# A decoder layer on one core: its opening cut into feature pairs, its last two products turned to tokens on partitions

## The chip, the cores and the metric

The kernel runs on one core of a Trainium2 chip. The metric is the device time of one launch in microseconds (us), with all inputs in HBM at its start and the result in HBM at its end.

## The reference, cut to what matters

One layer over 512 tokens and 1024 features, in float32:

```python
h = rms_norm(x, norm_mix[i])
proj = (h @ w_in[i])                       # 3840 columns: attention A, HGRN2 B, MoBA C
x = x + concat(ya, yb, yc) @ w_out[i]
x = x + GatedMLP(DWConv3(rms_norm(x, norm_ffn) @ w_up)) @ w_down
x = x + sigmoid(rms_norm(x, norm_ple) @ w_pg) * (p[i] @ w_pe)
return rms_norm(x, norm_final)
```

w_pe is 256 x 1024 and w_pg 1024 x 1024. rms_norm divides a token's row by the root of its mean square and multiplies by a gain per feature.

## The kernel before, in words

Each product is made of three: operands are split into a rounded part (`w_hi`, `h_hi`) and the remainder (`w_lo`, `h_lo`), and hi x hi, hi x lo and lo x hi are summed in a PSUM bank (lines 466 to 468). ScalarE (ACT) makes the hi parts, VectorE (DVE) the lo parts. Weights come in "units" of 512 KB (8 blocks of 128 x 128, `UNITS`): SyncE loads a unit into one of three `raw` slots, when the unit three before has its lo part; ACT and DVE split it two units ahead; TensorE (PE) runs its 24 matmuls of 512 columns (tokens); DVE "takes" the bank. Features lie on partitions: a unit's output is 128 features x 512 tokens.

**Order.** Every engine runs a list written out by hand, `beside_unit(u)` on ACT and DVE. Units 0 to 29 are w_in, 30 to 37 w_out, 38 to 81 w_up (in a loop), 82 to 105 w_down, 106 and 107 w_pe, 108 to 115 w_pg. PE uses two accumulator banks in turn, so unit u waits until unit u-2 is taken.

**Opening.** SyncE loads x in four tiles of 128 tokens, then units 0, 1, 2. PE transposes x in 32 transposes of 128 x 128 (L650); DVE and ACT copy them to `x_t`. ACT makes 8 `h_hi` (L839) and DVE 8 `h_lo` (L1167) for all of x, and unit 0 runs. ACT sums the squares of each token's row (L1033, four times), DVE takes the root of them in 13 small steps (`rstd_of_rows`, L1183 to L1195) and spreads it on a diagonal (L1200); PE turns this into `r_row` during unit 1 (L486). Only then can unit 0 be taken (L1217): the norm's root multiplies the product. The first four units (z) each need a take, three activations and three DVE steps (L1272 and on).

**Last stage.** Units 106 and 107 (`p @ w_pe`) give 8 banks, which ACT copies to `pe_out`. For each of the 8 w_pg units, 128 features x 512 tokens: DVE multiplies with `r_row` (L1217), ACT takes the sigmoid (L912), DVE multiplies with `pe_out` and adds to `x_t` (L1312, L1314), PE transposes the result to rows (L778, four transposes in the next unit), DVE multiplies with the final gain (L1320), and ACT squares four pieces (L971). The last unit runs in two halves of 256 tokens (`take_half` and on). Then, by halves: mean, Ln, Exp, three DVE steps, and the scaling of whole rows by DVE (L1591) and ACT (L1140), and four output DMAs of 512 KB (L456).

## Time and profile before

| | |
|---|---|
| median of 3 runs | 750.8 us (748.54, 750.8, 750.8) |
| the profiled execution, its own time | 747.16 us |
| its span, first to last instruction | 745.4 us |
| around the span | 1.76 us |
| mean granted TensorE clock | 0.993 |
| busy: PE, weight loads, DVE, ACT, POOL | 723.8, 592.6, 453.2, 314.2, 122.4 us |

Times in the rows below are us from the start of the span. A timeline row is start, duration, engine, line, operation, out<-in, count, and in brackets how long the engine had been idle and who released it. The granted clock is 1.00 at TensorE's 2.4 GHz and 0.50 at 1.2 GHz. An operation's duration ends when its result is there; a pipelined engine starts the next one some 0.1 us earlier (ACT, DVE), and TensorE 0.16 us earlier.

### The profile page before, as it was taken

To read this page: it belongs to the slowest core of one execution; us is meant where nothing else is said; L and a number is where in the kernel's file an instruction comes from. 1 tells how busy PE (TensorE), PEld (TensorE's weight loads), DVE (VectorE), ACT (ScalarE), POOL (GpSimd) and SP (SyncE) were. 2 spreads that over 40 slices of the span, in tenths; PEclk is the share of its full clock that TensorE was granted. 3 is DMA by queue.
4 is the path that set the end of the run, shared out by engine and by line. 5 is a ranking of instruction groups with operands and counts; after the bars stand their busy time and mean duration, and the time that the engine had idled before them with its cause. 6 is when DMAs were issued, how large, how long until landed. Compare 5 with 4: busy or idle time off the path is not lost.

```text
span 745.4 us, 10529 instructions
## 1 busy us (share of the span) xinstructions
PE 723.8 (97%) x3935; PEld 592.6 (80%) x3935; DVE 453.2 (61%) x705; ACT 314.2 (42%) x545; POOL 122.4 (16%) x99
## 2 busy tenths in 40 slices
PE   5999999998999999999999999999999999999993
PEld 4778777877888878778888888888888888888883
DVE  4754779748866645576767676676763333324555
ACT  7652214255665634444333343433332223226344
POOL 1030000025655432201011101101110001000000
PEclk9999999999999999999999999999999999999998
DMA  8333221312222102333332323333215332333202
GB/s 263 113 89 112 58 58 57 118 53 85 86 86 86 58 29 85 113 107 92 97 102 85 112 84 107 90 94 103 85 49 163 98 105 79 99 113 113 86 0 114
DMA packets 121745, 69.44 MB, mean 93 GB/s; under 512 B 2658, under 2 KB 118450, under 8 KB 121706
## 3 DMA queue, kind: packets, MB, share of 16 engines
q1 hardware_dynamic: 119982, 65.72, 29.4%
q10 hardware_dynamic: 1724, 3.19, 1.3%
q8 instruction: 26, 0.43, 0.2%
q14 instruction: 13, 0.11, 0.0%
HBM read 66.77 MB, written 2.13 MB: 92 GB/s over the span
## 4 chain that ended last, share of the span: by engine, by line
PE 88%; DVE 5%; ACT 3%; issue 1%; DMA 1%; SPq 0%; POOL 0%; DVEq 0%; ACTq 0%
PE bank L466 26%; PE bank L468 26%; PE bank L467 26%; PE bank L506 2%; PE bank L606 2%; DVE w_lo L1161 2%; PE bank L588 2%; PE bank L574 1%; DMA raw<-in_w_in 1%; ACT w_hi L834 1%; PE bank L576 1%; DVE h_lo L1167 1%; DVE x_t L1252 1%; PE bank L540 1%; ACT scratch L852 1%
## 5 line engine op out<-in xcount | busy, mean ns | idle before, releaser
L466 PE MATMUL bank<-h_hi,w_hi 128*128 128x512 f32 (+1 forms) x664 | 264.3, 398 | 2.6 <-DVE h_lo L1167 2.6
L468 PE MATMUL bank<-h_hi,w_lo 128*128 128x512 f32 (+1 forms) x664 | 257.8, 388 | 0.0
L467 PE MATMUL bank<-h_lo,w_hi 128*128 128x512 f32 (+1 forms) x664 | 257.7, 388 | 0.0
L834 ACT ACTIVATE w_hi<-raw 128x1024 fp32r<-128x1024 f32 (+1 forms) x116 | 120.8, 1042 | 288.2 <-PE bank L468 288.1
L1161 DVE TENSOR_TENSOR w_lo<-raw,w_hi 128x1024 fp32r<-128x1024 f32 (+1 forms) x116 | 144.7, 1247 | 113.0 <-ACT w_hi L834 112.8
L466 PEld LDWEIGHTS bank<-h_hi,w_hi 128*128 128x128 f32 x664 | 125.1, 188 | 28.6 <-DVE w_lo L1161 2.8
L468 PEld LDWEIGHTS bank<-h_hi,w_lo 128*128 128x128 f32 x664 | 125.1, 188 | 26.2
L467 PEld LDWEIGHTS bank<-h_lo,w_hi 128*128 128x128 f32 x664 | 125.3, 189 | 24.2 <-issue 1.0
L1647 POOL TENSOR_SCALAR probs<-probs,row_inv 128x512 f32<-128x512 f32 (+3 forms) x48 | 66.0, 1379 | 148.4 <-DVE row_inv L1432 148.1
L466 PE MATMUL bank<-act_hi,w_hi 128*128 128x512 f32 x176 | 68.6, 389 | 0.0
L468 PE MATMUL bank<-act_hi,w_lo 128*128 128x512 f32 x176 | 68.5, 389 | 0.0
L467 PE MATMUL bank<-act_lo,w_hi 128*128 128x512 f32 x176 | 68.5, 389 | 0.0
L1217 DVE TENSOR_TENSOR scratch<-bank,r_row 128x512 f32<-128x512 f32 x54 | 37.3, 690 | 45.5 <-PE bank L468 43.7
L1655 POOL TENSOR_TENSOR conv_v<-conv_g,conv_v 128x512 f32<-128x512 f32 x22 | 28.3, 1288 | 213.1 <-DVE conv_v L1290 213.1
L1625 POOL TENSOR_TENSOR sumsq<-sumsq,scratch 128x512 f32<-128x512 f32 x14 | 18.1, 1295 | 146.8 <-ACT scratch L852 146.8
L985 ACT ACTIVATE probs<-probs,row_min 128x512 f32<-128x512 f32 (+3 forms) x48 | 27.0, 563 | 35.2 <-DVE row_min L1426 35.0
L1426 DVE CUSTOM_DVE_ANT_0 probs<-bank,bias 128x512 f32<-128x512 f32 (+3 forms) x48 | 23.5, 489 | 27.9 <-PE bank L576 18.5
L839 ACT ACTIVATE h_hi<-x_t,vec_cols 128x512 fp32r<-128x512 f32 x24 | 16.6, 719 | 53.3 <-DVE x_t L1252 53.3
L467 PEld LDWEIGHTS bank<-act_lo,w_hi 128*128 128x128 f32 x176 | 33.0, 188 | 6.9
L468 PEld LDWEIGHTS bank<-act_hi,w_lo 128*128 128x128 f32 x176 | 33.0, 188 | 6.8
L466 PEld LDWEIGHTS bank<-act_hi,w_hi 128*128 128x128 f32 x176 | 33.0, 188 | 6.8
L993 ACT ACTIVATE probs_t<-bank 128x512 f32<-128x512 f32 (+3 forms) x48 | 20.6, 429 | 9.5 <-PE bank L588 8.9
(186 smaller groups left out, 791.7 us busy)
## 6 DMA issues: line engine op xcount, KB each, us to landing
raw<-in_w_up SPq DMA_DIRECT2D x44, 512.0 KB, 3.6
raw<-in_w_in SPq DMA_DIRECT2D x30, 512.0 KB, 3.7
raw<-in_w_down SPq DMA_DIRECT2D x16, 512.0 KB, 3.2
raw<-in_w_out SPq DMA_DIRECT2D x8, 512.0 KB, 3.3
raw<-in_w_pg SPq DMA_DIRECT2D x8, 512.0 KB, 3.3
bias<-bias_table ACTq DMA_DIRECT2D x6, 512.0 KB, 3.7
raw<-in_w_down SPq DMA_DIRECT2D x8, 384.0 KB, 2.8
x_rows<-in_x SPq DMA_DIRECT2D x4, 512.0 KB, 5.8
```

What stands on the lines that cost most here:

```text
L466: pe.matmul(bank, hi, x_hi, start=first, stop=False)
L467: pe.matmul(bank, hi, x_lo, start=False, stop=False)
L468: return pe.matmul(bank, lo, x_hi, start=False, stop=last)
L834: act.activation(w_hi[:, u % SPLIT, 0:nk * ncol], raw[:, u % RAW, 0:nk * ncol], ACT.Copy)\
L985: act.activation(probs[:, n % PROBS, 0:keys], probs[:, n % PROBS, 0:keys], ACT.Exp, scale=-1.0, bias=row_min[:, n:n + 1], accum_out=row_su ...
L993: act.activation(probs_t[:, n % TURNED, 0:keys], turned[n % 2][:, 0:keys], ACT.Copy).then_inc(probs_t_ready, 1)
L1161: dve.tensor_tensor(w_lo[:, u % SPLIT, 0:nk * ncol], raw[:, u % RAW, 0:nk * ncol], w_hi[:, u % SPLIT, 0:nk * ncol].bitcast(F32), ALU.subtr ...
L1217: return dve.tensor_tensor(out, bank, r_row[:, :], ALU.mult)
L1426: dve.tensor_tensor_reduce(out=probs[:, n % PROBS, 0:keys], in0=score[n % 2][:, 0:keys], in1=bias[:, pair % 2, head % 2, SEQ - keys:SEQ], ...
L1625: pool.tensor_tensor(sumsq[:, :], sumsq[:, :], scratch[:, 2 + f % 2, :], ALU.add).then_inc(sumsq_ready, 1)
L1647: pool.tensor_scalar(probs[:, n % PROBS, 0:keys], probs[:, n % PROBS, 0:keys], row_inv[:, n:n + 1], None, ALU.mult)\
L1655: pool.tensor_tensor(conv_v[:, j % 3, :], conv_g[:, j % 3, :], conv_v[:, j % 3, :], ALU.mult).then_inc(prod_ready, 1)
```

## The change

**Opening.** x is loaded in four pairs of feature blocks (all 512 tokens x 256 features, rows of 1 KB in HBM), each followed by the same two blocks of units 0, 1 and 2 (128 KB each). The identity moves to ACT's DMA queue. TensorE first runs 7 matmuls on a zeroed tile, then transposes pair 0, runs two more of those, and then, pair by pair, the products of units 0, 1, 2 side by side in three banks, with the transposes of the next pair between. `h_hi` and `h_lo` are made straight from the transposes' banks. Groups 0 to 7 go over four banks instead of two (`bank_of`, `frees`). The row squares, all four, come on ACT after the last pair, then the splits of units 3, 4 and 5, then `r_row` (in unit 3's last block). The conv transposes and the bias look-up move two units later.

**Last stage.** w_pe and w_pg become moving operands and the activations stationary: output is 128 tokens x 512 features. 8 pieces of w_pe (6 matmuls each) are each followed by the transposes of one `x_t` block into `y_rows` (`turn_rows`), copied by DVE and ACT in turn. The norm's root is then one number per token and partition, so the sigmoid applies it as its scale and reads the bank directly. w_pg is loaded as 8 units of 256 x 512, five of which have split tiles of their own (`pg_hi`, `pg_lo`). 8 tiles `g` follow: tokens g % 4, feature half g // 4; the last in two halves of 256 columns. There are no transposes in this stage and the squares are taken from `y_rows`. Roots of tokens 0 to 383 are found on DVE in 13 steps (`root_of`), that of the last 128 with Ln and Exp as before. Rows leave in four DMAs, the last split in two. The gain row is loaded at unit 85 instead of unit 111, into `conv_v`'s place.

The diff, cut to its core; of the parts that replace others mostly the added lines stand:

```diff
-for _f in range(KT):
-    _unit("w_pg", 0, KT, _f * P)
-    _group("ple", _f)
+for _c in range(2):
+    for _k0 in range(0, KT, 2):
+        _unit("w_pg", _k0, 2, _c * 512, 512)
...
+def bank_of(group):
+    return group % 4 if group < WIDE else group % 2
+def frees(group):
+    return None if group < 4 else group - 4 if group < WIDE + 2 else group - 2
+def split_at(u):
+    return {1: None, 2: None, 3: 6, 4: 7, 5: 8, 6: None}.get(u, u + 2)
...
-            for t in range(TT):
-                sp.dma_start(x_rows[:, t, :], a["x"][0, t * P:(t + 1) * P, :]).then_inc(x_in[t], 16)
-                if t == 0:
-                    sp.dma_start(square[:, 0:P], a["c_square"][:, 0:P]).then_inc(ident_in, 16)
-            load_unit(0)
-            load_unit(1)
+            for j in range(PAIRS_K):
+                cols = slice(2 * j * P, (2 * j + 2) * P)
+                sp.dma_start(x_rows[:, :, cols], a["x"][0, :, cols].rearrange("(t p) c -> p t c", p=P)).then_inc(x_in[j], 16)
+                for u in range(FIRST):
+                    name, _, _, c0, ncol = UNITS[u]
+                    sp.dma_start(raw[:, u, cols].rearrange("p (k c) -> p k c", c=ncol),
+                                 w_dram[name][cols, c0:c0 + ncol].rearrange("(k p) c -> p k c", p=P)).then_inc(piece_in[u][j], 16)
...
+                    sp.wait_ge(act_ready, FT)
+                    sp.dma_start(gain_row, a["norm_final"].rearrange("(o d) -> o d", o=1).to_broadcast([P, D]))\
                       .then_inc(gain_in, 16)
...
+            def keep_warm(count):
+                for _ in range(count):
+                    pe.matmul(banks[2][:, :], q_both[:, 0, 1, 0:P], q_both[:, 0, 0, :], start=True, stop=True)
...
+            def turn_x(j):
+                pe.wait_ge(x_in[j], 16)
+                for k in (2 * j, 2 * j + 1):
+                    if j >= 2:
+                        pe.wait_ge(h_lo_ready, k - 3)
+                        pe.wait_ge(x_kept_dve if k % 2 else x_kept_act, j - 1)
+                    for t in range(TT):
+                        mm = pe.transpose(banks[4 + k % 4][:, t * P:(t + 1) * P], x_rows[:, t, k * P:(k + 1) * P], ident)
+                    mm.then_inc(x_turned, 1)
...
+            pe.wait_ge(blank_ready, 1)
+            keep_warm(7)
...
+            turn_x(0)
+            keep_warm(2)
+            for j in range(PAIRS_K):
+                first_products(0, j)
+                first_products(1, j)
...
+                if j < PAIRS_K - 1:
+                    turn_x(j + 1)
+                first_products(2, j)
...
+                    if u == 3 and k == 7:
                         pe.wait_ge(square_in, 16)
                         spread_row()
+                    if u == 4 and k == 5:
                         turn_conv()
+                    if u == 5 and k == 5:
                         look_up_bias()
...
+            def turn_rows(f):
+                pe.wait_ge(x_ready, KT + f + 1)
+                if f >= 2:
+                    pe.wait_ge(rows_act if f % 2 else rows_dve, f // 2)
                 for t in range(TT):
+                    mm = pe.transpose(turned[f % 2][:, t * P:(t + 1) * P], x_t[:, f, t * P:(t + 1) * P], ident)
+                mm.then_inc(rows_turned, 1)
...
+            for n in range(PIECES):
+                c, t = n // TT, n % TT
+                u = PE_UNITS + c
+                if t == 0:
+                    pe.wait_ge(wlo_ready, u + 1)
+                if c:
+                    pe.wait_ge(pe_kept, n - 3)
+                tokens = slice(t * P, (t + 1) * P)
+                for k in range(2):
+                    cols = slice(k * 512, (k + 1) * 512)
+                    mm = token_products(banks[PE_BANK[t]][:, :], p_hi[:, k, tokens], p_lo[:, k, tokens],
+                                        w_hi[:, u % SPLIT, cols], w_lo[:, u % SPLIT, cols], k == 0, k == 1)
+                mm.then_inc(unit_done if t == TT - 1 else pe_done, 1)
+                if n == 4:
+                    sum_tokens()
+                turn_rows(n)
...
+                for cols in (slice(0, 512),) if g < PIECES - 1 else (slice(0, 256), slice(256, 512)):
+                    for k in range(KT):
+                        w = 4 * c + k // 2
+                        if t == 0 and k % 2 == 0:
+                            pe.wait_ge(wlo_ready, PG + w + 1)
+                        if g == 0:
+                            wait_h(2, k)
+                        hi, lo = pg_tiles(w)
+                        at = slice(k % 2 * 512 + cols.start, k % 2 * 512 + cols.stop)
+                        mm = token_products(pg_bank(g, cols), h_hi[:, k, tokens], h_lo[:, k, tokens], hi[:, at], lo[:, at],
+                                            k == 0, k == KT - 1)
+                    mm.then_inc(pg_done, 1)
...
+            for j in range(PAIRS_K):
+                first_gain(2 * j)
+                first_split(0, j)
+                first_gain(2 * j + 1)
+                first_split(1, j)
+                first_split(2, j)
+                act.wait_ge(h_lo_ready, 2 * j + 1)
+                act.activation(x_t[:, 2 * j, :], banks[4 + 2 * j % 4][:, :], ACT.Copy).then_inc(x_kept_act, 1)
...
             for t in range(TT):
+                square_rows(t)
+            split_hi(3)
+            split_hi(4)
+            split_hi(5)
             act.wait_ge(filled, 1)
+            spread()
...
+            def sigmoid_of(g, n, cols):
+                act.wait_ge(pg_done, n + 1)
+                if g >= 3:
+                    act.wait_ge(y_added, g - 2)
+                act.activation(conv_g[:, g % 3, cols], pg_bank(g, cols), ACT.Sigmoid, scale=r_tok[:, g % TT:g % TT + 1])\
+                   .then_inc(sig_ready, 1)
...
+            whole, left, right = slice(0, 512), slice(0, 256), slice(256, 512)
+            for n in range(PIECES):
+                keep_pe(n)
+                if n == 5:
+                    root_of_tokens()
+                if n % 2:
+                    keep_rows(n)
+                else:
+                    split_pg(n // 2)
+            act.preload_act_table(ACT.Sigmoid)
+            act.wait_ge(tok_newton, 3)
+            for g in range(PIECES - 1):
+                sigmoid_of(g, g, whole)
+                if g < TT:
+                    split_pg(4 + g)
+                square_of(g, g, whole)
+            scale_rows(0, y_root, 1)
+            scale_rows(1, y_root, 1)
+            sigmoid_of(PIECES - 1, PIECES - 1, left)
+            scale_rows(2, y_root, 2)
+            square_of(PIECES - 1, PIECES - 1, left)
+            sigmoid_of(PIECES - 1, PIECES, right)
             act.preload_act_table_set("natural_log_exp_and_others")
+            square_of(PIECES - 1, PIECES, right)
+            t = TT - 1
+            act.wait_ge(mean_ready, 1)
+            act.activation(stat[:, 2, t:t + 1], stat[:, 1, t:t + 1], ACT.Ln).then_inc(y_ln, 1)
+            act.wait_ge(y_ln, 1)
+            act.activation(stat[:, 2, t:t + 1], stat[:, 2, t:t + 1], ACT.Exp, scale=-0.5).then_inc(y_guess, 1)
+            scale_rows(t, y_root, 3)
...
+            for j in range(PAIRS_K):
+                first_lo_x(2 * j)
+                first_split(0, j)
+                first_lo_x(2 * j + 1)
+                first_split(1, j)
+                first_split(2, j)
+                dve.tensor_copy(x_t[:, 2 * j + 1, :], banks[4 + (2 * j + 1) % 4][:, :]).then_inc(x_kept_dve, 1)
+            split_lo(3)
             rstd_of_rows()
             dve.wait_ge(ident_in, 16)
             diagonal()
+            split_lo(4)
+            split_lo(5)
...
+                dve.tensor_tensor(conv_g[:, g % 3, cols], conv_g[:, g % 3, cols], pe_out[:, t, here], ALU.mult).then_inc(gated, 1)
+                dve.wait_ge(gated, n + 1)
+                dve.tensor_tensor(y_rows[:, t, here], y_rows[:, t, here], conv_g[:, g % 3, cols], ALU.add).then_inc(y_added, 1)
...
+            whole, left, right = slice(0, 512), slice(0, 256), slice(256, 512)
+            for n in range(0, PIECES, 2):
+                keep_rows(n)
+                split_pg(n // 2)
+            root_of_tokens()
+            for g in range(PIECES - 1):
+                add_gated(g, g, whole)
+                if g < TT:
+                    split_pg(4 + g)
+                if g == 1:
+                    dve.wait_ge(gain_in, 16)
+                if 1 <= g <= TT:
+                    gain_rows(g - 1)
+                if g == 5:
+                    root_of(0, 2)
+                    finish_rows(0, y_root, 1)
+                    finish_rows(1, y_root, 1)
+            root_of(2, 3)
+            add_gated(PIECES - 1, PIECES - 1, left)
+            add_gated(PIECES - 1, PIECES, right)
+            finish_rows(2, y_root, 2)
```

`token_products` issues (x_hi, m_hi), (x_hi, m_lo), (x_lo, m_hi) with x stationary. `keep_pe`, `keep_rows` and `split_pg` are one copy of 128 x 512, one of 128 x 512 and one split of 128 x 1024. `sum_tokens` is 4 float32 matmuls of one column. `square_of` is one ACT square with its sum, `finish_rows` and `scale_rows` scale 512 columns of a token tile on DVE and ACT, `gain_rows` multiplies 512 columns with the gain.

## Rows read from the trace of the kernel before

**Rows 1.** Page, part 4: who holds the chain that ended last.
```profile
PE 88%; DVE 5%; ACT 3%; issue 1%; DMA 1%; SPq 0%; POOL 0%; DVEq 0%; ACTq 0%
```

**Rows 2.** Timeline of the opening: start, duration, engine, line, operation.
```profile
4.45 1.06 ACT L1033 ACTIVATE scratch<-x_rows 128x1024 f32<-128x1024 f32 x1 [2.44 <-DMA x_rows<-in_x]
...
4.66 1.97 PE L650 MATMUL bank<-square,x_rows 128*128 128x128 f32 x8 [4.66 <-DMA square<-in_c_square]
...
5.42 0.19 ACT L1033 ACTIVATION_READ_ACCUMULATOR scratch<-x_rows 128x1 f32 x1
...
10.72 1.29 PE L650 MATMUL bank<-square,x_rows 128*128 128x128 f32 x8
...
14.65 0.76 PE L466 MATMUL bank<-h_hi,w_hi 128*128 128x512 f32 x1 [2.64 <-DVE h_lo L1167]
```

**Rows 3.** Chain of waits, opening: start and length of a product.
```profile
15.84 0.43 PE bank L468
...
20.11 0.23 PE bank L467
```

**Rows 4.** Stages of the opening: engines' busy time, then PEclk, DMA share, GB/s.
```profile
15.00:16.00 1.00, 1.00 (x3) 0.78 (x3) 1.00 (x3) 1.00 (x3) 0.00 (x0) 0.50 1.01 264
...
17.70:18.50 0.80, 0.80 (x4) 0.65 (x3) 0.80 (x3) 0.80 (x2) 0.00 (x0) 0.82 0.09 26
```

**Rows 5.** Groups of instructions by shape, 0 to 30 us.
```profile
L1167 DVE SCALAR_TENSOR_TENSOR h_lo<-x_t,vec_cols,h_hi 128x512 fp32r<-128x512 f32 x8 | 5.4, 748 | 0.1
...
L834 ACT ACTIVATE w_hi<-raw 128x1024 fp32r<-128x1024 f32 x5 | 5.2, 1050 | 1.2 <-PE bank L468 1.2
...
L839 ACT ACTIVATE h_hi<-x_t,vec_cols 128x512 fp32r<-128x512 f32 x8 | 5.0, 708 | 0.0
...
L1161 DVE TENSOR_TENSOR w_lo<-raw,w_hi 128x1024 fp32r<-128x1024 f32 x4 | 4.9, 1221 | 0.9 <-ACT w_hi L834 0.8
```

**Rows 6.** Timeline of VectorE, opening.
```profile
21.05 0.17 DVE L1183 TENSOR_SCALAR stat<-stat 128x4 f32<-128x4 f32 x1
...
23.43 0.69 DVE L1200 TENSOR_TENSOR scratch<-square,stat 128x512 f32<-128x512 f32 x1
...
26.92 0.69 DVE L1217 TENSOR_TENSOR scratch<-bank,r_row 128x512 f32<-128x512 f32 x1 [1.67 <-ACT r_row L856]
...
31.31 0.68 DVE L1217 TENSOR_TENSOR scratch<-bank,r_row 128x512 f32<-128x512 f32 x1
...
52.07 0.69 DVE L1217 TENSOR_TENSOR b_kq<-bank,r_row 128x512 f32<-128x512 f32 x1 [2.57 <-PE bank L468]
```

**Rows 7.** DMA view, 0 to 25 us in 40 slices: GB/s.
```profile
GB/s 0 0 51 275 389 230 171 270 331 269 328 407 413 355 342 345 346 350 365 365 348 340 249 139 270 286 319 231 66 2 0 0 0 0 0 35 229 341 225 9
```

**Rows 8.** Timeline of VectorE at the start of w_down.
```profile
561.40 0.69 DVE L1330 TENSOR_TENSOR act_lo<-conv_v,act_hi 128x512 fp32r<-128x512 f32 x1
...
565.25 1.23 DVE L1161 TENSOR_TENSOR w_lo<-raw,w_hi 128x1024 fp32r<-128x1024 f32 x1 [3.15 <-ACT w_hi L834]
```

**Rows 9.** Timeline of the last stage, VectorE, ScalarE and SyncE.
```profile
733.78 0.42 DVE L1550 TENSOR_TENSOR conv_g<-bank,r_row 128x256 f32<-128x256 f32 x1 [0.16 <-PE bank L468]
...
734.67 1.28 ACT L1147 ACT_TABLE_LOAD   x1
...
738.78 0.17 DVE L1573 TENSOR_REDUCE stat<-parts 128x2 f32<-128x16 f32 x1 [0.60 <-ACT scratch L971]
...
740.31 1.15 ACT L1140 ACTIVATE y_rows<-y_rows,stat 128x1024 f32<-128x1024 f32 x1 [0.68 <-DVE stat L1586]
...
741.10 0.81 SPq L456 DMA_DIRECT2D out<-y_rows  x2
```

**Rows 10.** Chain of waits, last stage: row sum, and four transposes.
```profile
679.19 0.86 PE bank L481 x2
...
695.06 0.44 PE bank L778 x4
```

**Rows 11.** Output DMAs of line 456, from issue to landing.
```profile
DMA to landing us min/median/max: 2.6/3.1/3.5
```

More of the change, by code:

```diff
@@ L123 @@
 PROBS = 5
+FIRST = 3
+PAIRS_K = KT // 2
+WIDE = 8
 TURNED = 5
@@ L388, in wait_taken, with pg_tiles, pg_bank @@
                 eng.wait_ge(acc_taken, rnd * UP_ROUND + sum(g[0] != "x" for g in GROUPS[:group + 1]))
+        def pg_tiles(w):
+            if w < OWN_PG:
+                return pg_hi[:, w, :], pg_lo[:, w, :]
+            return w_hi[:, (PG + w) % SPLIT, :], w_lo[:, (PG + w) % SPLIT, :]
+        def pg_bank(g, cols):
+            return banks[6 if g == PIECES - 1 and cols.start else g % TT][:, cols]
         def tot_at(level):
@@ new lines, in turn_x, with first_products @@
+            def turn_x(j):
[7 more added lines that the diff above has]
+                    mm.then_inc(x_turned, 1)
+            def first_products(u, j):
+                if j < PAIRS_K - 1:
+                    pe.wait_ge(first_lo, FIRST * j + u + 1)
+                else:
+                    pe.wait_ge(wlo_ready, u + 1)
+                for k in (2 * j, 2 * j + 1):
+                    if u == 0:
+                        wait_h(0, k)
+                    mm = products(banks[bank_of(u)][:, :], u, k, P, 0, h_hi[:, k, :], h_lo[:, k, :], k == 0, k == KT - 1)
+                if j == PAIRS_K - 1:
+                    mm.then_inc(unit_done, 1)
@@ L1047, in _, with first_gain, first_split @@
-            act.wait_ge(x_kept_act, TT)
-            act.wait_ge(x_kept_dve, TT)
-            act.wait_ge(vec_ready, 1)
-            for f in range(KT):
-                gain_x(0, f)
-            square_rows(3)
-            split_hi(1)
+            def first_gain(k):
+                act.wait_ge(x_turned, k + 1)
+                act.activation(h_hi[:, k, :], banks[4 + k % 4][:, :], ACT.Copy, scale=vec_cols[:, k:k + 1]).then_inc(h_hi_ready, 1)
+            def first_split(u, j):
+                cols = slice(2 * j * P, (2 * j + 2) * P)
+                act.wait_ge(piece_in[u][j], 16)
+                act.activation(w_hi[:, u, cols], raw[:, u, cols], ACT.Copy)\
+                   .then_inc(first_hi if j < PAIRS_K - 1 else whi_ready, 1)
@@ L1221, in take @@
                 kind, i, unit = GROUPS[group]
-                bank = acc[group % 2]
+                bank = banks[bank_of(group)]
                 dve.wait_ge(unit_done, rnd * UP_ROUND + (unit + 1))
@@ L1542, in _ @@
                         split_act((u - UP) // 2 - 1, rnd)
[L1543 removed]
+            for u in range(DOWN, PE_UNITS + 1):
                 beside_unit(u)
[L1547 to L1551 removed]
```

459 lines of the change are left out of this document (202 added, 257 removed).

## The prediction, made before the changed kernel was run

> **What bounds the kernel now.** I read the chain that ended last first: TensorE holds 88% of it [rows 1]. Between the opening and the tail, products follow each other every 0.227 us without a gap, 24 to a unit (5.44 us). The change neither adds nor removes a product, and the middle (units 6 to 105) keeps its code, so the time can only move in three ways: when TensorE reaches a fixed point in the middle, what it does from the first w_pe product to its last, and what follows that.
>
> So I read both ends as timelines. In the opening the reader is to see that x's first tile is there at 4.45, yet the first product starts at 14.65 [rows 2], and costs 0.43 us instead of 0.23 [rows 3]: TensorE is granted half its clock, 0.50, until about 18.0 (a mean of 0.82 over 17.7 to 18.5) [rows 4]. In the last stage four transposes of 0.44 stand between a w_pg unit's products; from the take of the last half at 733.78 to the last scaling's end at 741.46 lie 7.7 us, and the output DMAs end the span at 745.4 [rows 9, 10].
>
> **The fixed point.** VectorE takes unit 5 at 52.07 [rows 6], so TensorE starts unit 6 at about 51.9. This is 14.65 + 6 x 5.44 = 47.3, plus some 8 cold products at 0.2 each (1.6), plus 3.0 for root spread, conv transposes and bias look-up, which the change moves but keeps.
>
> **The opening, step by step.** A piece of 256 columns is priced at 0.42 (the half at 733.78 [rows 9]), one of 1024 by [rows 5].
>
> - x's pair 0 is 512 KB like x's first tile, so it lands at 4.4, and the three pieces of weights behind it by 5.6, at some 330 GB/s [rows 7]. The seven blank matmuls cost 7 x 0.43 = 3.0 from about 1.6, under this DMA. Four transposes end at 5.5, ACT's h_hi (0.71) at 6.2, its weight piece at 6.6, DVE's h_lo (0.75) at 7.0 and w_lo piece at 7.3. First product: 7.4.
> - 72 products of units 0 to 2 are 16.3. Between them lie 24 transposes of pairs 1 to 3, no longer ahead: 0.11 each [rows 10] and a little per group, 3.1. Waits for h_lo of the next pair: some 0.5. TensorE has done units 0 to 2 at 27.3. ACT and DVE need 2.7 and 3.3 us a pair, TensorE 5.0, so these hide.
> - ACT ends its part of pair 3 at 24.0 (transposed at 21.8) and now has the four squares in one run: 4 x (1.06 + 0.19 - overlap) = 4.8 [rows 2], to 28.8. Only behind them stands w_hi of unit 3 (1.05, to 29.9) and then DVE's w_lo (1.22): unit 3 can start at 31.1. **TensorE waits 3.8 us.** The squares were free before, under the DMA; now they stand ahead of a split that TensorE needs. (The load of unit 3 waits for unit 0's last lo piece at 23.1 and lands by 27: it is not what is late.)
> - Unit 3 with the root spread is 5.44 + 1.1, to 37.6. DVE's root is ready in time: 13 steps at 0.2 (21.05 to 23.43) and the diagonal 0.69 [rows 6] after 31.1 give 34.3. But unit 4 needs bank 0, hence r_row (0.6) and the take of unit 0 (0.69): it starts at 38.3, 0.7 later.
> - Units 4 and 5 with conv and look-up: 10.9 + 1.9. Unit 6 starts at 51.1. Its banks come free in time: takes of z units followed each other in 4.4 us (26.92 to 31.31 [rows 6]) while behind, less than 5.44. w_lo of unit 6 comes behind take 2, at about 48.8: 2.3 us of slack.
>
> 51.1 against 51.9 is a gain of 0.8, from: 7.3 earlier start, 1.6 of cold products saved, against 3.1 transposes, 0.5, 3.8 and 0.7 of waits.
>
> **The clock.** Before, eight transposes took 1.97 at first and 1.29 at 10.72 [rows 2]: the clock had risen. TensorE then idled 2.6 us, and its first products were at half rate [rows 3, 4]. The blank matmuls and transposes should raise it before 7.4. But the new wait is 3.8 us, longer than the one that lost it. I take it as lost again: some 8 products at 0.2 more, 1.6 us, bounded by 0 (not lost) and 3.2 (twice as long at half rate). The opening then is 0.8 **slower** than before (51.1 + 1.6 against 51.9). The Trainium skill (TensorE: Matmul & The Clock Gate, HAM oscillation — how this bites in real kernels) states that a long enough gap between bursts of matmuls throttles the array, and that each burst after it starts cold. By it the wait costs 1.6, without it nothing. The trace agrees on the opening's own gap [rows 2, 3].
>
> **The middle.** SyncE now waits for the last act_lo, done at 562.1, before it loads the gain row (512 KB), with the loads of units 86 to 88 behind it in its queue. Unit 86 then lands near 567 (1 MB at 330 GB/s and some 2 us of issue and latency), and its w_lo comes near 569.5 instead of 565.25 [rows 8]. Splits run two units ahead; TensorE starts unit 86 near 573.4. Hidden by 4 us of lead; without it the cost would be those 4.
>
> **The last stage.** Bounded from TensorE's first w_pe product at 673.6, at before's time. Eight pieces of 6 x 0.23 + 0.48 for the transposes, and 0.9 for the sum [rows 10], reach 689.4; six tiles of 5.44, transposes gone from between them, 722.1. Output transposes are 32 instead of 36 (the last block was turned twice). The token root on ACT and DVE, 1.2 in all, is ready at 691, before tile 0 ends. ACT's copies and splits per two pieces are 2.8 us against TensorE's 3.7, hidden; the split tiles come a piece ahead.
>
> From tile 5 on the chain leaves TensorE: sigmoid 0.7, two DVE steps 1.4, square 0.8 (725.2); root of tokens 0 to 255, 13 steps, 2.6 (727.8); two scalings 1.4 (729.2); then only tile 6's two DVE steps (730.6), its square (731.4), the root of tile 2, 2.6 (734.0), the left half's two steps (734.9), its square, and the right half's sigmoid at 735.3, though TensorE ended at 733.2. Behind it the table load 1.28 (737.0) [rows 9], the right half's square (737.4), and mean to root as before, 1.55 (738.78 to 740.31): 739.0. Scaling is 512 columns, 0.75, not 1024: 739.8, against 741.46. Last issue at 740.2, landing 2.6 to 3.1 later [rows 11] as only 512 KB in all is left: the span ends 743.1 against 745.4, a gain of 2.3. If products next to transposes cost more (0.56 per group of four, 0.23 throughout) it is 1.4; if the right half could follow TensorE's end at once, 1.9 earlier, it is 4.2.
>
> **Sum.** -0.8 + 1.6 - 2.3 = -1.5: the profiled execution's 747.16 becomes 745.7. The median of the runs lies 3.6 above it, so I carry the difference to the median: 750.8 - 1.5 = **749.3**. A run of this kernel can tell from no change about 0.3%, 2.25 us.
>
> **Rivals.**
>
> - *The clock survives the wait at unit 3.* For: TensorE was busy for 20 us ahead of it. Against: 2.6 us were enough before. Then -3.1: 747.7.
> - *The wait at unit 3 is small* because ACT is done earlier than I add up, or the squares fit beside. Then up to 3.8 and the clock's 1.6 come off, less the banks' wait for r_row, which hangs on the same squares: -4 to -6, about 745.5. Against: ACT's order is fixed, and its inputs come from TensorE's own transposes.
> - *The blank matmuls don't raise the clock in time.* For: they last 3.0 us, and before the clock rose only 3.3 us into the products [rows 4]. Opening at half rate: 1.6 for products, 0.7 for transposes, so +0.8: 751.6.
> - *The opening starves for data* (the other side). x comes in 1 KB rows and 16 transfers of 512 and 128 KB. TensorE wants pair 3 at 20.6, with 3.3 MB loaded: from 1.9 on that is 175 GB/s. At 140 GB/s it comes at 25.2, 4.6 later, pair 0 another 1.5 later: +4 or so, 753 to 755. It decides from 175 down. Against: weights in 512-byte rows ran at 340 to 413 GB/s, and the lowest slice, amid x, was 170 [rows 7]. The Trainium skill (DMA: Bandwidth & Descriptors, Bandwidth) asks for 1 MiB a transfer and puts one of 64 KB at 138 GB/s; by that figure this rival's +4 would come true. The trace doesn't agree so far: loads of 512 KB ran at the rates above.
> - *The new last stage gives nothing.* For: its DVE chain sets the end, not TensorE, and each step has a wait. If every link cost 0.1 more (about 50 links), the 2.3 is 0 or less... then +0.8 with the clock lost: 751.6 to 753.
>
> **How the numbers follow.** Forecast (clock lost, tail gained) 0.42; clock survives 0.25; small wait 0.10; blank matmuls fail 0.10; starved 0.05; tail gives nothing 0.08. Each case has an error of some 1.5 us. Faster by over 0.3% (below 748.55): most of the two that gain, and a quarter of the forecast, 0.38. Slower by over 0.3%: starved, part of the tail and of the blank case, 0.11. The rest, 0.51. Range 745.8 to 752.2: it holds forecast, surviving clock and failed blanks, and leaves out starvation and the best of the small wait.
>
> **What would show it.** In the new profile: the first product near 7.4, spacing 0.23 from the first; TensorE idle 3 to 4.5 us before unit 3, with VectorE's w_lo as its releaser and ACT's four squares just ahead; a granted clock of 0.50 and 0.43 spacing behind it; unit 6 at 51 to 53. At the end, 5.44 per w_pg tile with no idle TensorE between them, DVE busy without gaps in `root_of`, the right half's sigmoid 2 us after its products, last scaling 6 to 6.5 us after TensorE's end. I am wrong if TensorE waits elsewhere in the opening (a bank, a DMA), if the wait at unit 3 is under 2 us, or if the w_pg tiles wait for splits.

## The result, and the profile of the changed kernel

The changed kernel's median is 752.84 us (751.73 to 753.07, six runs), that of the kernel before beside it 750.43: 1.0045 times as long, 95% interval 1.0031 to 1.0059. It is 0.45% slower; 749.3 was forecast, and the range ended at 752.2. The profiled execution took 751.73 us, its span is 749.9, against 747.16 and 745.4 before: 4.5 more.

The page's chain (answers to [rows 1]), engines and then lines:

```profile
PE 92%; DVE 4%; ACT 2%; issue 1%; ACTq 0%; DVEq 0%
```

TensorE still sets the time, now with 92% of the chain. So I compare when it reaches the same work in both traces. These are differences of start times, after minus before, taken from the two timelines:

| work | before | after | later by | gained or lost in the stretch |
|---|---|---|---|---|
| take of unit 7 | 62.95 | 64.27 | 1.3 | opening +1.3 |
| take at w_in's slot 17 | 176.89 | 178.29 | 1.4 | 0.1 |
| the next take | 195.79 | 198.79 | 3.0 | **+1.6** |
| first take of the w_up loop's steady run | 341.05 | 344.41 | 3.4 | 0.4 |
| last take of w_up | 553.21 | 556.57 | 3.4 | 0.0 |
| first w_pe product | 673.59 | 680.45 | 6.9 | **+3.5** |
| end of the span | 745.4 | 749.9 | 4.5 | last stage -2.4 |

The last stage gained what was forecast (2.3), the opening lost 1.3 where 0.8 was forecast. The surprise is the middle, which was priced at nothing: 5.5 us. The profiled execution was the fastest of the six (751.73; the others 752.66 to 753.07), so the table shows this kernel at its best.

**Opening.** Timeline of the changed kernel, TensorE, ScalarE and VectorE (answers to [rows 2, 6]):

```profile
1.99 3.35 PE L684 MATMUL bank<-q_both 128*128 128x512 f32 x7 [1.99 <-DVE q_both L1269]
...
8.55 0.50 PE L505 MATMUL bank<-h_hi,w_hi 128*128 128x512 f32 x1 [0.72 <-DVE w_lo L1582]
...
25.67 1.07 ACT L1092 ACTIVATE scratch<-x_rows 128x1024 f32<-128x1024 f32 x1
...
30.28 2.23 ACT L911 ACTIVATE w_hi<-raw 128x1024 fp32r<-128x1024 f32 x2
...
32.63 0.50 PE L505 MATMUL bank<-h_hi,w_hi 128*128 128x512 f32 x1 [3.26 <-DVE w_lo L1275]
...
40.22 0.47 PE L505 MATMUL bank<-h_hi,w_hi 128*128 128x512 f32 x1 [0.93 <-DVE scratch L1331]
```

The reader sees the two waits of the forecast: 3.26 us at unit 3, with ACT's squares (from 25.67 on, the first of four is shown) ahead of the split that starts at 30.28, and 0.93 at unit 4 for the take of unit 0. But the first product starts at 8.55, not 7.4.

**Middle, the step near 178.** Timeline of TensorE, the kernel before and then the changed one; the stages' columns are busy times, then PEclk, DMA share, GB/s:

```profile
176.11 1.75 PE L606 MATMUL bank<-probs_t,v_tok 128*64 128x128 f32 x28 [1.99 <-ACT probs_t L993]
```

```profile
177.51 3.00 PE L646 MATMUL bank<-probs_t,v_tok 128*64 128x128 f32 x28 [2.01 <-ACT probs_t L1053]
```

```profile
178.00:180.00 2.00, 2.00 (x22) 2.00 (x20) 0.96 (x4) 1.67 (x4) 0.60 (x1) 0.50 0.23 46
```

The same 28 small matmuls behind the same idle 2 us take 1.75 us at full clock and 3.00 at a granted 0.50 (178 to 180).

**Middle, w_down.** Groups of TensorE in it (570 to 670), before and then after; the columns are count, busy us, mean ns:

```profile
L468 PE MATMUL bank<-act_hi,w_lo 128*128 128x512 f32 x147 | 57.2, 389 | 0.0
L466 PE MATMUL bank<-act_hi,w_hi 128*128 128x512 f32 x146 | 56.9, 390 | 0.0
L467 PE MATMUL bank<-act_lo,w_hi 128*128 128x512 f32 x146 | 56.8, 389 | 0.0
```

```profile
L505 PE MATMUL bank<-act_hi,w_hi 128*128 128x512 f32 x143 | 56.6, 396 | 0.0
L507 PE MATMUL bank<-act_hi,w_lo 128*128 128x512 f32 x142 | 56.1, 395 | 0.0
L506 PE MATMUL bank<-act_lo,w_hi 128*128 128x512 f32 x142 | 56.1, 395 | 0.0
```

No idle time in either, the clock is 1.00 in both, yet each product takes 6 ns more, and fewer fit in the same 100 us. Single starts in the timelines lie 0.2267 us apart before and 0.2333 after; 528 products by 0.0066 are the 3.5 us.

**Last stage.** Its timeline in the changed kernel (answers to [rows 9]), and the landing of the last two output DMAs (to [rows 11]):

```profile
742.35 0.46 ACT L1217 ACTIVATE conv_g<-bank,r_tok 128x256 f32<-128x256 f32 x1
742.82 1.28 ACT L1257 ACT_TABLE_LOAD   x1
...
744.65 0.16 DVE L1746 TENSOR_REDUCE stat<-last_parts 128x1 f32<-128x3 f32 x1 [0.28 <-ACT scratch L1226]
...
746.09 0.72 ACT L1233 ACTIVATE y_rows<-y_rows,stat 128x512 f32<-128x512 f32 x1 [0.61 <-DVE stat L1755]
...
746.83 0.81 SPq L495 DMA_DIRECT2D out<-y_rows  x2
```

```profile
DMA to landing us min/median/max: 2.0/2.2/2.3
```

Counted from the first w_pe product, the right half's sigmoid comes at 61.9 (forecast 61.7), the last scaling ends at 66.4 (66.2), the span at 69.45 (69.5).

### The profile page after: what moved, and what is told of

Its sections match the earlier page's. It is cut to its first block, busy times and chain, and to the rows that moved or that the text cites. A ratio compares the mean times of both kernels' runs of the same rounds, so it can differ in the third digit from the quotient of the medians.

```text
span 749.9 us, 10563 instructions
## 1 busy us (share of the span) xinstructions
PE 731.2 (98%) x3947; PEld 593.1 (79%) x3947; DVE 450.9 (60%) x728; ACT 313.1 (42%) x513; POOL 122.9 (16%) x99
## 3 DMA queue, kind: packets, MB, share of 16 engines
q10 hardware_dynamic: 1868, 3.26, 1.3%
## 4 chain that ended last, share of the span: by engine, by line
PE 92%; DVE 4%; ACT 2%; issue 1%; ACTq 0%; DVEq 0%
PE bank L505 26%; PE bank L507 25%; PE bank L506 25%; PE bank L646 2%; PE bank L546 2%; PE bank L832 2%; PE bank L834 2%; PE bank L833 2%; PE bank L628 2%; PE bank L614 1%; PE bank L616 1%; PE bank L580 1%; ACT scratch L1092 0%; PE bank L600 0%; PE bank L842 0%
## 5 line engine op out<-in xcount | busy, mean ns | idle before, releaser
L505 PE MATMUL bank<-h_hi,w_hi 128*128 128x512 f32 x592 | 237.3, 401 | 5.1 <-DVE w_lo L1275 3.3
L507 PE MATMUL bank<-h_hi,w_lo 128*128 128x512 f32 x592 | 231.1, 390 | 0.0
L506 PE MATMUL bank<-h_lo,w_hi 128*128 128x512 f32 x592 | 230.9, 390 | 0.0
L911 ACT ACTIVATE w_hi<-raw 128x1024 fp32r<-128x1024 f32 (+1 forms) x105 | 109.2, 1040 | 271.3 <-PE bank L507 262.6
L1275 DVE TENSOR_TENSOR w_lo<-raw,w_hi 128x1024 fp32r<-128x1024 f32 (+1 forms) x105 | 130.8, 1247 | 111.0 <-ACT w_hi L911 111.0
L505 PEld LDWEIGHTS bank<-h_hi,w_hi 128*128 128x128 f32 x592 | 111.2, 188 | 31.3 <-DVE w_lo L1275 3.7
L507 PEld LDWEIGHTS bank<-h_hi,w_lo 128*128 128x128 f32 x592 | 111.1, 188 | 23.9
L506 PEld LDWEIGHTS bank<-h_lo,w_hi 128*128 128x128 f32 x592 | 111.3, 188 | 21.7 <-issue 1.0
L507 PE MATMUL bank<-act_hi,w_lo 128*128 128x512 f32 x176 | 69.5, 395 | 0.0
L506 PE MATMUL bank<-act_lo,w_hi 128*128 128x512 f32 x176 | 69.5, 395 | 0.0
L916 ACT ACTIVATE h_hi<-x_t,vec_cols 128x512 fp32r<-128x512 f32 x16 | 11.6, 724 | 52.4 <-DVE x_t L1366 52.4
```

The lines of the kernel that those rows point to most:

```text
L505: pe.matmul(bank, hi, x_hi, start=first, stop=False)
L506: pe.matmul(bank, hi, x_lo, start=False, stop=False)
L507: return pe.matmul(bank, lo, x_hi, start=False, stop=last)
L911: act.activation(w_hi[:, u % SPLIT, 0:nk * ncol], raw[:, u % RAW, 0:nk * ncol], ACT.Copy)\
L1275: dve.tensor_tensor(w_lo[:, u % SPLIT, 0:nk * ncol], raw[:, u % RAW, 0:nk * ncol], w_hi[:, u % SPLIT, 0:nk * ncol].bitcast(F32), ALU.subtr ...
```

## The experiments

Thirteen kernels ran, in four groups on three chips. The kernel before, run beside each group, had medians of 748.73 to 749.23 (750.43 beside the changed kernel), so ratios are what to compare. A ratio stands with its 95% interval. "Take of unit 7" and "first w_pe product" are from each run's profile.

### Chance, or one of the two parts?

**before_again**: no edit.

> The kernel before, unchanged, profiled a second time. The changed kernel reached its first w_pe product 6.9 us later than the kernel before (680.45 against 673.59), only 1.3 of it from the opening; 1.6 came in one step near 178 us, where 28 small products behind an idle 2.01 us ran at a granted clock of 0.50, and 3.5 came evenly over w_down, whose products follow each other every 0.233 us instead of 0.227. Theory 1: both are chances of a single execution. Then this second profile of the same kernel shows a span up to 5 us longer than 745.4, with a 0.233 spacing in w_down or a burst at half clock somewhere in the middle. Theory 2: both belong to the changed kernel. Then this profile has 0.227 in w_down, no burst at half clock after the first 20 us and its first w_pe product at 673.6, within 0.5.

Span 746.3. w_down at 0.2267, so the slow spacing is no chance. But the 28 small matmuls were at half clock here as well:

```profile
175.48 2.23 PE L606 MATMUL bank<-probs_t,v_tok 128*64 128x128 f32 x28 [1.99 <-ACT probs_t L993]
```

The take behind them came 1.5 later. So theory 1 holds for the step near 178 and theory 2 for w_down. Over all profiles of this study the clock fell at this idle time of 1.99 to 2.02 us (at its end or up to 1.4 us into the small matmuls) in 6 of 15, in kernels with and without the change: a lottery of 1.6 us that every version plays.

The opening of this profile holds another such case. TensorE idled 3.32 us ahead of its first product, and then ran its first 22 products at 0.23 us and a granted clock of 1.00 (14 to 16 us). In the other seven profiles with this opening, before's among them, the idle time there was shorter, 2.44 to 2.74, and six to eight products at 0.43 followed, at once or after a few at 0.23.

**last_stage_alone**: the diff's last stage, with before's opening.

> The opening of before, the last stage of the change. Theory: the two parts add up, and the last stage is worth what the profiles show between the first w_pe product and the end of the span, 71.8 against 69.45, so 2.4 faster than before, ratio 0.997. Its first w_pe product comes at 673.6 as in before if the slower middle hangs on the opening (or on the instructions' place behind it); if the slower middle comes with the last stage (the gain row's load at unit 85, the other tiles), the product spacing of w_down is 0.233 here too, the first w_pe product comes at 677, and the kernel is 1 slower than before. Rival: the new last stage gives nothing, ratio 1.000.

Ratio 1.0023 (1.0009 to 1.0036): slower, and the first w_pe product at 678.67, with the spacing of 0.2333 in w_down. The alternative in the expectation came true: the slow middle belongs to the last stage's edits. Averaged over 10 us each, the spacing turns in 550 to 560 us, where w_down begins:

```
540: 0.2267   550: 0.230   560: 0.2333   570: 0.2333   ...   670: 0.2333
```

**opening_alone**: the diff's opening, with before's last stage.

> The opening of the change, the last stage of before. Theory: the wait at unit 3 (3.3 us) makes the opening a loss, and the two parts add up: the changed kernel is 2.4 slower at the median with a last stage that gains 2.4, so the opening alone costs 4.8, ratio 1.0064, with 1.3 us of it visible at unit 7 and the rest in the middle. Rival: the middle's loss was chance of one profile; then the opening alone costs 1.3 (2.5 where the clock falls in the wait), ratio 1.002 to 1.0035.

Ratio 1.0018 (1.0007 to 1.0030), w_down at 0.2267. The theory (1.0064) falls, the rival is nearer, at its lower edge: by these runs the opening costs some 1.3 us and nothing behind it. TensorE waited 3.25 at unit 3, and here its clock fell (a granted 0.63 in 33 to 35 us, 0.51 in 35 to 37); the take of unit 7 came at 65.77, 1.5 later than in the changed kernel's profile, where the clock stayed up.

### Where the tiles lie

The edits of the last stage that reach back to w_down are these:

```diff
-        sb("after_small", [P, 40])
+        r_tok = sb("r_tok", [P, TT])
+        last_parts = sb("last_parts", [P, TT, 3])
+        sb("after_small", [P, 40 - 4 * TT])
```

The filler gives up just the 64 bytes that the new tiles hold. But each tile is rounded up to 32 bytes: 32 + 64 + 96 = 192 instead of 160. In the built programs act_hi begins at byte 138752 of each partition before and at 138784 after, and so all tiles from the mixers' on; x_t, h_hi, raw, w_hi and w_lo stay. Before the change all these starts are multiples of 256 bytes (h_hi at 33024, w_hi at 78080), and so are the distances between a product's two operands.

**before_shifted**:

```diff
-        sb("after_small", [P, 40])
+        sb("after_small", [P, 48])
```

> The kernel before with 8 unused columns (32 bytes) more ahead of the mixers' and the MLP's tiles, nothing else. Runs so far: the spacing of 0.2333 us in w_down came with the last stage of the change (in the profile of that alone, not in that of the opening alone), from the first product that reads act_hi on, 20 us ahead of any instruction that the last stage changes. What the last stage does change there is the place of the tiles: two new small tiles and a filler that was cut by their size, but each is rounded up to 32 bytes, so all tiles behind them start 32 bytes later. Theory (place): a moving operand that starts 32 bytes off a multiple of 64 costs 0.2333 a product instead of 0.2267. Then this kernel has 0.2333 in w_down, 528 products by 0.0066 = 3.5 us, and 0.4 more in the mixers and w_out: 3.9 slower than before, ratio 1.005. Rival: the spacing comes from something else of the last stage (the program's size, the gain row's load); then the spacing here is 0.2267 and the ratio 1.000.

Ratio 1.0053 (1.0033 to 1.0074). The take of unit 7 is at 64.18 (1.2 later than before), the first w_pe product at 678.73 (5.1 later): 3.9 came between them. Shown: 32 unused bytes cost as much as the whole loss (the changed kernel's ratio is 1.0045). The group in w_down reads as the changed kernel's:

```profile
L466 PE MATMUL bank<-act_hi,w_hi 128*128 128x512 f32 x142 | 56.2, 396 | 0.0
```

**after_aligned**:

```diff
-        sb("after_small", [P, 40 - 4 * TT])
+        sb("after_small", [P, 16])
```

> The changed kernel with the filler ahead of the mixers' tiles cut by 8 columns more, so that those tiles start where they did before. Theory (place): w_down gets its 0.2267 back (-3.5), the mixers and w_out 0.4, and the 120 w_pg products that read the five own split tiles 0.8: 4.7 faster than the changed kernel, so about 748.1, or 0.2% faster than before; the first w_pe product comes 3.9 earlier, w_pg tiles follow each other in 5.44 instead of 5.54. Rival: no change of spacing, the time stays at 752.8.

748.13, ratio 0.9985 (0.9973 to 0.9997) where the changed kernel had 1.0045. w_down is at 0.2267 again and the w_pg tiles' sigmoids follow each other in 5.44 us throughout, against up to 5.60:

```profile
715.24 0.69 ACT L1217 ACTIVATE conv_g<-bank,r_tok 128x512 f32<-128x512 f32 x1 [2.54 <-PE bank L834]
720.68 0.69 ACT L1217 ACTIVATE conv_g<-bank,r_tok 128x512 f32<-128x512 f32 x1 [2.54 <-PE bank L834]
```

**last_stage_aligned**: last_stage_alone with the same edit.

> The opening of before with the last stage of the change, and the tiles where they were before. Theory (place): the last stage alone came out 0.23% slower only because it moved the tiles; without that its gain shows: 2.4 from the profiles of the ends and 0.8 from the w_pg products, so 3.2 faster than before, ratio 0.9957. Rival: the tail's gain was paid back somewhere else as well, ratio 0.998 or more.

745.05, ratio 0.9942 (0.9919 to 0.9965; one of its six runs, at 1473 us, is far off and left out). From the first w_pe product (674.99) to the end of the span (743.6) are 68.6, 3.2 less than before. The last stage is a gain of 0.6% by the timed runs and of 3.2 us, 0.4%, by the profiles. Set against after_aligned, on the same chip, this run gives a second price of the opening: 748.13 against 745.05, so 3.1 us, where opening_alone gave 1.3.

**before_shifted_64**: the filler at 56 columns.

> The kernel before with 16 unused columns (64 bytes) more ahead of the mixers' and the MLP's tiles, where the run with 8 columns cost 0.53%. Theory (half step): only an odd number of 32 bytes hurts a moving operand. Then w_down stays at 0.2267 and the ratio is 1.000, within 0.2%. Rival: those tiles have to start at a multiple of 128 bytes, as they did before (138752 is 1084 x 128; with 64 more it isn't one); then w_down has 0.2333 or more and the ratio is 1.005 or more.

Neither. Ratio 1.0016 (1.0002 to 1.0031), w_down at 0.2288: a third of the price.

**weights_shifted**:

```diff
+        sb("before_raw", [P, 8])
         raw = sb("raw", [P, RAW, 1024])
...
-        sb("after_small", [P, 40])
+        sb("after_small", [P, 32])
```

> The kernel before with raw, w_hi, w_lo and the small tiles 32 bytes later, and everything from the mixers' tiles on in its place. In it the stationary operand (the weights) of all 2500 products is off by 32 bytes and the moving one is not. Theory: only the moving operand's place counts; spacing 0.2267 everywhere, ratio 1.000 to 1.001 (ACT and DVE read and write moved tiles too, which the run may show). Rival: a stationary operand off by 32 bytes costs as well, in the weight loads; then the spacing is above 0.2267 in w_up and w_down alike, or the weight loads' mean is longer with the spacing unchanged.

763.7, ratio 1.0179 (1.0156 to 1.0201). My theory (only the moving operand counts) falls: with the weights 32 bytes later and the moving operands in place every 512-column product is at 0.2333, in w_up as in w_down. The weight loads' own rows don't show it, their mean is 188 ns as before.

```profile
L469 PE MATMUL bank<-h_hi,w_lo 128*128 128x512 f32 x144 | 57.0, 396 | 0.0
```

**all_shifted**: all tiles 32 bytes later.

```diff
-        sb("before_x", [P, 32])
+        sb("before_x", [P, 40])
```

> The kernel before with every tile of it 32 bytes later, so that the moving and the stationary operand of each product are both off. So far the spacing was 0.2333 instead of 0.2267 with the moving one alone off (in w_down), and 0.2333 as well with the stationary one alone off (all products, 15 us of the span). Theory 1 (two reads, each with its price): the prices add, spacing 0.240 everywhere, some 2500 products by 0.013, 30 us slower or more, ratio 1.04. Theory 2 (one price, whichever operand starts off its place): spacing 0.2333 everywhere, ratio 1.018 to 1.022. Theory 3 (what costs is that the two operands stand differently to each other): with both off by the same 32 bytes the spacing is 0.2267 and the ratio 1.000.

749.62, ratio 1.0002 (0.9989 to 1.0016), 0.2267 in w_up and in w_down. Theory 3 holds: not where an operand starts, but how far the moving and the stationary one lie apart. A distance of whole 256 bytes costs nothing, one off by 32 either way costs 0.0066 us a product, one off by 64 some 0.0022. No run has a distance that is an odd multiple of 128, and what in the chip does this, the runs don't tell.

### What TensorE waits for in the opening

**squares_in_gaps** (tiles as in the changed kernel):

```diff
+                if j in (1, 2):
+                    square_rows(2 * j - 2)
+                    square_rows(2 * j - 1)
...
-            for t in range(TT):
-                square_rows(t)
             split_hi(3)
```

> The changed kernel with one edit: ACT squares the rows in its idle time inside the pair loop (two behind pair 1, two behind pair 2), no longer between pair 3 and the split of unit 3. Theory: the squares are what TensorE waits for at unit 3. Then its wait there falls from 3.3 us to under 0.5, the 0.9 at unit 4 goes too, the take of unit 7 comes near 60.2 instead of 64.27, and the kernel is 4.2 faster than the changed one (5.2 if the clock also fell in the wait in most runs): 747.6 to 748.6. Rival 1: the next split waits for its data instead (the w_hi of unit 5 waited 0.43 for its load), then 1 to 2 of the gain is lost. Rival 2: a later wait absorbs it, and the gain at unit 7 is under 1.

The theory falls in half, rival 1 was nearer, and larger than I put it. ScalarE had squared everything by 22.7, and then stood:

```profile
29.01 1.06 ACT L911 ACTIVATE w_hi<-raw 128x1024 fp32r<-128x1024 f32 x1 [3.23 <-DMA raw<-in_w_in]
```

```profile
31.38 0.79 PE L505 MATMUL bank<-h_hi,w_hi 128*128 128x512 f32 x1 [2.02 <-DVE w_lo L1277]
```

TensorE's wait fell only from 3.26 to 2.02 us, and its clock fell in that (0.54 in 33 to 35 us), so the take of unit 7 came at 64.61. Ratio 1.0023 (1.0012 to 1.0034) against the changed kernel's 1.0045: in the timed runs the moved squares are worth some 0.2%, though the take of unit 7 is no earlier in this profile. Two things stood side by side before unit 3: the squares, and unit 3's load. It is issued at 24.9, when unit 0's last quarter is split, and is there 4.0 later.

**opening_mended**: the tiles in place, the squares in the gaps, the spread in unit 3's fifth block, and the loads of units 3 to 5 in quarters:

```diff
+            for j in range(PAIRS_K):
...
+                for u in range(FIRST, 2 * FIRST):
...
+                    if j < PAIRS_K - 1:
+                        sp.wait_ge(first_lo, FIRST * j + u - FIRST + 1)
+                    else:
+                        sp.wait_ge(wlo_ready, u - FIRST + 1)
+                    sp.dma_start(raw[:, u - FIRST, cols]..., w_dram[name][cols, c0:c0 + ncol]...)
```

> The changed kernel, tiles in place as in the run above, and three edits of the opening: the row squares in ACT's gaps behind pairs 1 and 2; units 3 to 5 loaded in quarters, each as soon as its quarter of the raw slot is free, instead of whole when unit 0's last quarter is split; the root's spread in unit 3's fifth block instead of its eighth. The squares alone gained nothing at unit 7 (take at 64.61 against 64.27), because the load of unit 3, issued at 24.9, landed only at 28.8: two things of the same length stood before unit 3. Theory: with both gone TensorE waits under 0.7 us at unit 3 and not at all at unit 4, the clock stays up, the take of unit 7 comes at 59.1 to 59.8, 4.5 to 5 earlier than in the changed kernel and 3.2 to 3.9 earlier than before, and the kernel is 743 to 744, ratio to before 0.992. Rival 1: the quarters disturb the loads behind them and a later unit waits for its data; the gain at unit 7 is under 2. Rival 2: the gain at unit 7 is there but given back in the mixers; the first w_pe product shows it.

742.45, ratio 0.9919 (0.9897 to 0.9940), the fastest kernel here, 0.8% under before and, by the two ratios, 1.3% under the changed one. The take of unit 7 is at 61.00, 3.3 earlier than in the changed kernel and nothing of it is given back. The time is as expected (0.992), the take of unit 7 is 1.2 to 1.9 later than expected, because unit 3 still waits 1.44 for its last quarter:

```profile
27.95 2.95 ACT L926 ACTIVATE w_hi<-raw 128x1024 fp32r<-128x1024 f32 x3 [2.63 <-DMA raw<-in_w_in]
```

```profile
30.32 0.50 PE L516 MATMUL bank<-h_hi,w_hi 128*128 128x512 f32 x1 [1.44 <-DVE w_lo L1292]
```

**quarters_alone**: this without the moved squares.

> The mended opening without the moved squares: units 3 to 5 loaded in quarters, the spread early, but ACT's four squares again between pair 3 and the split of unit 3. With the squares alone moved the wait at unit 3 was still 2.02 us, because the load came late. Theory: two things stand in parallel before unit 3, and this leaves the squares; TensorE waits 3.3 us at unit 3 (w_lo released by w_hi behind the squares), may lose its clock there (0 to 3 us), and the take of unit 7 comes at 63 to 66, 2 to 5 later than in the mended kernel's 61.0. Ratio to before 0.995 to 0.999. Rival: the quarters did all of the mending; take of unit 7 at 61 to 62.

As the theory has it: 3.26 at unit 3, the clock at 0.50 until about 38, take of unit 7 at 65.64. The wait of 0.93 at unit 4 is gone with the earlier spread. For the wait at unit 3 it takes both edits: 2.02 with the squares moved, 3.26 with the quarters, 1.44 with both. The timed runs are kinder to each alone: this kernel's ratio is 0.9948 (0.9926 to 0.9971), just below the forecast range, against after_aligned's 0.9985, so some 0.4%, beside the 0.2% of the squares and 0.7% for all together. That the edits are worth more together than one by one is not shown in the time.

**mended_no_blanks**: opening_mended without the 7 and 2 blank matmuls.

> The mended kernel without the 7 and 2 matmuls on a zeroed tile ahead of its first products. Theory: they are what raises the clock by the first product; without them the transposes and the first 8 products or more run at a granted clock of 0.50, spacing 0.43, each 0.2 more, until some 3 us of work are behind them: the take of unit 7 comes 1.5 to 2.5 later than 61.0 and the kernel is 1.5 to 2.5 slower than the mended one's 742.45. Rival: the eight transposes raise the clock by themselves, or the lost time is taken up by the wait at unit 3 (1.44 us in the mended kernel); then the difference is under 0.7.

In the profile the transposes start 0.6 earlier than in opening_mended (4.87 against 5.44) and the first product 0.1 earlier (7.95 against 8.06), but 12 products follow each other in 0.43 us:

```profile
8.54 0.63 PE L517 MATMUL bank<-h_lo,w_hi 128*128 128x512 f32 x1
8.96 0.63 PE L518 MATMUL bank<-h_hi,w_lo 128*128 128x512 f32 x1
```

The take of unit 7 is at 65.01, 4.0 later, of which 12 x 0.2 = 2.4 are these products and the rest a clock that fell in a wait of 1.81 at unit 3. The time of this profiled run, 746.07, was the longest of its four, though (743.2, 743.8, 744.3 the others), and the ratios, 0.9912 (0.9890 to 0.9935) here and 0.9919 there, can't be told apart. What the blank matmuls are worth in the time stays open. That they bring the first products to full rate is shown by the spacing: 0.23 from the start in all six profiles with them, 0.43 for 12 products in the one without. The granted clock doesn't show it, its rows read 1.00 there in both.

## Why the prediction was wrong, by its own steps

- **"The middle (units 6 to 105) keeps its code", and so costs nothing: this step failed.** The order of TensorE's work there is indeed unchanged, but its operands were moved by 32 bytes against the weights. By the first w_pe product this cost 3.9 us (3.5 in w_down, 0.4 in mixers and w_out), and 0.8 more in the w_pg products that read `pg_hi` and `pg_lo`. Without it the ratio is 0.9985, and 749.3 to 750.8 was forecast, 0.998. That this agrees is partly luck: two terms of the sum were too small, and they cancel. With the tiles in place the last stage gains 3.2 instead of 2.3 (4.2 by timed runs), and the opening loses 3.1 by the timed runs of the same chip instead of 0.8.
- **The profiled executions.** Another 1.6 of the 4.5 us between the two spans is the clock's fall near 178, a chance in every version, and no effect of the change. In return this execution kept its clock at unit 3. An estimate for the five others: after_aligned's span of 746.4, in which the clock was lost for 2.9 us at unit 3 and kept near 178, plus the 3.9 and 0.9 of the moved tiles is 751.2, and their spans are 750.9 to 751.3.
- **From the profile to the median.** The forecast carried 3.6 us from before's profiled execution to a median of 750.8 out of three runs. Before's later runs, 73 beside the four groups, have medians of 748.7 to 749.2, with most runs near 748.5 or near 750.8; the base was of the upper kind, and so were four of the six runs beside the changed kernel. Against the later medians the changed kernel's 752.84 is some 0.5% longer instead of 0.45%, an estimate across chips.
- **The gain row** was hidden, as said: w_lo behind its load came late (unit 86's started at 572.55, 3.1 us behind the forecast 569.5, no more than the 3.4 us by which everything there came later), TensorE never stood.
- **Opening, the start**: mis-sized. First product 7.4 forecast, 8.55 measured. The blank matmuls, which I laid "under this DMA", run to 5.3 and hold up transposes that could start at 4.9 (mended_no_blanks); I also had the first four transposes done by 5.5, but the eight took until 7.4, at half rate still.
- **Opening, the pair loop**: mis-sized. 19.9 forecast (16.3, 3.1, 0.5), 20.8 measured (8.55 to 29.37).
- **Opening, the wait at unit 3**: mechanism right, size 3.8 against 3.26. But "(The load of unit 3 ... is not what is late)" was wrong: it was issued at 24.95, 1.8 later than I had it, took 4.3 and landed at 29.25, only 1.0 us before the squares let ScalarE go on (30.28). Whoever had acted on my account would have moved the squares alone, and the wait falls by that only from 3.26 to 2.02 (squares_in_gaps).
- **Opening, unit 4**: 0.7 forecast, 0.93 measured.
- **The clock in that wait**: taken as lost at 1.6, bounded by 0 and 3.2. In the profiles with a 3.25 us wait it cost 0 (the changed kernel), 1.5 (opening_alone) and 2.9 (after_aligned against the changed kernel, 67.13 to 64.27). So the loss ran from nothing to nearly the upper bound, and one profile can't settle it. The argument that a longer wait than 2.6 us loses the clock was weak: before_again kept it through 3.32. The Trainium skill (TensorE: Matmul & The Clock Gate, HAM oscillation — how this bites in real kernels) has each burst after a long enough gap start cold; the traces agree in three of four waits of 3.25 us, not in the changed kernel's own, nor in before_again's 3.32.
- **The opening in sum**: 0.8 slower forecast; 1.3 by the two first profiles, 1.9 by the mean take of unit 7 (63.8 in the seven profiles of the old opening with its weights in place, 65.7 in three of the new), 0.18% or 1.3 us by the timed runs of opening_alone, 3.1 us by those of after_aligned against last_stage_aligned. Its size stays open between these; all of them are more than forecast.
- **The last stage**: 2.3 forecast, 2.3 to 2.4 measured in the changed kernel, but with the w_pg tiles at up to 5.60 instead of 5.44; 3.2 with the tiles in place. Two errors cancel here. In the changed kernel TensorE ends 60.3 after the first w_pe product (59.6 forecast), and the end comes as forecast. In after_aligned TensorE ends at 59.5, the right half's sigmoid comes at 61.1 (61.7 forecast) and the span ends at 68.6 (69.5): the chain behind tile 5 was priced 0.9 too long.
- **The rivals**: the "other side" ended there by none of the ways I had named. Data starvation did not come (TensorE waited for no load in the pair loop).

## What to carry to other kernels

A change that adds a tile moves every tile behind it. Before pricing unchanged code at nothing, compare the start addresses of what TensorE reads, and keep each moving operand a multiple of 256 bytes from its stationary one, the distance that cost nothing here; if a spacing changes evenly with no idle time and at the full clock, look there first. When a wait is removed on paper, ask what is second behind it in parallel, and price that one too: here the moved squares and the loads in quarters left 2.02 and 3.26 us of the wait by themselves, and 1.44 together. In the profiles the take of unit 7 was at 64.6 and 65.6 with one of them, where the clock fell as well, and at 61.0 with both, where it didn't. A clock that falls in some executions makes single profiles differ by 1.5 to 3 us; compare work between fixed points, and in several profiles.

## What the runs showed of the hardware that I had not expected

- The distance between a product's two operands in SBUF sets its rate: 0.2267 us at multiples of 256 bytes, 0.2288 when it is 64 more, 0.2333 when it is 32 more or less (128 x 128 by 512 columns). At 32 bytes it makes no difference to the spacing which of them is moved, and moving both by the same amount costs nothing (1.0002).
- TensorE's clock fell at an idle time of 1.99 to 2.02 us, with the same work ahead of it, in 6 of 15 profiles, and stayed up through one of 3.26 us in one of four. Ahead of the old opening's first product it stayed up through the longest of eight idle times, 3.32 us, and fell behind the other seven, 2.44 to 2.74. Between 2.0 and 3.3 us the length of the wait alone did not decide it.
